# A state-space stage that scans four tokens per step instead of two, and moves its rows through a scratch in HBM

## The reference

```
def s5_mixer(h, a_re, a_im, log_dt, b_re, b_im, c_re, c_im, d_skip, w_glu):
    u = h.astype(jnp.float32).reshape(B, L, N_GROUPS_2, SSM_GROUP)
    dt = jnp.exp(log_dt.astype(jnp.float32))[:, None]
    decay = jnp.exp(a_re * dt)
    ab_re = decay * jnp.cos(a_im * dt)
    ab_im = decay * jnp.sin(a_im * dt)
    ...
    bb_re = coef_re * br - coef_im * bim
    bb_im = coef_re * bim + coef_im * br
    bu_re = jnp.einsum('blgc,gpc->blgp', u, bb_re)
    bu_im = jnp.einsum('blgc,gpc->blgp', u, bb_im)
    ...
    _, _, x_re, x_im = lax.associative_scan(_complex_scan_op, (ar, ai, bu_re, bu_im), axis=1)
    y = (jnp.einsum('blgp,gcp->blgc', x_re, c_re.astype(jnp.float32))
         - jnp.einsum('blgp,gcp->blgc', x_im, c_im.astype(jnp.float32)))
    y = y.reshape(B, L, D) + d_skip.astype(jnp.float32) * u.reshape(B, L, D)
    g = jax.nn.gelu(y).astype(h.dtype)
    ga, gb = jnp.split(g @ w_glu, 2, axis=-1)
    return ga * jax.nn.sigmoid(gb)
```

## Time and profile before

| | |
|---|---|
| median of 3 runs | 2961.07 us (2959.12 to 2964.72) |
| the profiled execution | 2959.73 us |
| its span in the trace | 2957.9 us |
| TensorE busy | 2792.2 us, 94% of the span |
| VectorE busy | 1404.8 us, 47% |
| GpSimd busy | 860.2 us, 29% |
| ScalarE busy | 539.1 us, 18% |

### The profile page before, as it was taken

One profiled execution on the slowest core, in us unless ns is written; L12 is line 12 of the kernel. 1 busy time (PEld: TensorE's weight loads), 2 busy tenths in 40 slices (PEclk: granted clock), 3 DMA queues, 4 the chain that ended last, 5 costly groups with the idle time before them and its releaser, 6 DMA issues.

```text
span 2957.9 us, 28891 instructions
## 1 busy us (share of the span) xinstructions
PE 2792.2 (94%) x11348; PEld 1991.8 (67%) x11348; DVE 1404.8 (47%) x2231; ACT 539.1 (18%) x1019; POOL 860.2 (29%) x688
## 2 busy tenths in 40 slices
PE   8999999999999999999999899999994469999999
PEld 7888884755448888875446547888442124688888
DVE  6454312166526544232496434555317991466521
ACT  2000000111101000011121522222015430222200
POOL 5444320000324444410000323442014650344432
PEclk9999999999999999997799999999996679999999
DMA  6555321211125454221011002224210002122222
GB/s 225 169 171 167 100 96 57 71 52 48 43 86 167 164 171 160 86 72 43 27 59 57 29 29 72 93 92 124 68 52 16 0 1 86 58 92 92 83 79 68
DMA packets 222626, 253.37 MB, mean 86 GB/s; under 512 B 16328, under 2 KB 209180, under 8 KB 222364
## 3 DMA queue, kind: packets, MB, share of 16 engines
q1 hardware_dynamic: 207996, 199.32, 20.9%
q10 hardware_dynamic: 14496, 52.21, 5.1%
HBM read 249.41 MB, written 2.10 MB: 85 GB/s over the span
## 4 chain that ended last, share of the span: by engine, by line
PE 83%; DVE 12%; ACT 2%; issue 1%; POOL 1%; SPq 0%; DMA 0%; DVEq 0%; POOLq 0%
PE ps L612 36%; PE ps L668 13%; PE ps L1134 9%; PE ps L498 5%; PE ps L1600 4%; PE ps L2271 4%; DVE phase L2429 2%; PE ps L1161 1%; PE ps L1641 1%; PE ps L1653 1%; DVE phase L2414 1%; PE ps L893 1%; PE ps L1269 1%; DVE rs L1850 1%; DVE act_t L2371 1%
## 5 line engine op out<-in xcount | busy, mean ns | idle before, releaser
L612 PE MATMUL ps<-hT,ring 128*128 128x256 f32 x2816 | 653.6, 380 | 3.8 <-ACT hT L1039 1.4
L612 PEld LDWEIGHTS ps<-hT,ring 128*128 128x128 f32 x2816 | 534.2, 190 | 80.9 <-issue 4.1
L612 PE MATMUL ps<-phase,ring 128*128 128x256 f32 x2112 | 498.5, 379 | 0.4 <-DVE phase L561 0.4
L540 POOL TENSOR_TENSOR ring<-ring 128x512 f32<-128x512 f32 (+1 forms) x124 | 161.1, 1299 | 1005.8 <-DMA ring<-in_ffn_w 515.2
L612 PEld LDWEIGHTS ps<-phase,ring 128*128 128x128 f32 x2112 | 400.4, 190 | 54.7 <-issue 0.8
L668 PE MATMUL ps<-phase,ring 128*128 128x256 f32 x1848 | 400.6, 379 | 1.0 <-issue 1.0
L668 PEld LDWEIGHTS ps<-phase,ring 128*128 128x128 f32 x1848 | 350.7, 190 | 48.8 <-issue 1.4
L1134 PE MATMUL ps<-hT,ring 128*128 128x512 f32 x512 | 227.9, 599 | 3.1 <-ACT phase L1326 2.5
L1600 PE MATMUL ps<-hT,ring 128*128 128x512 f32 x448 | 198.2, 599 | 0.9 <-ACT hT L1039 0.9
L543 POOL TENSOR_TENSOR ring<-ring 128x512 f32<-128x512 f32 (+1 forms) x124 | 191.1, 1541 | 0.0
L694 DVE TENSOR_TENSOR act_t<-u,ps 128x256 f32<-128x256 f32 x176 | 73.4, 421 | 235.6 <-PE ps L612 235.3
(11 more groups left out here) (333 smaller groups left out, 3141.2 us busy)
## 6 DMA issues: line engine op xcount, KB each, us to landing
ring<-in_ffn_w SPq DMA_DIRECT2D x60, 1024.0 KB, 5.2
ring<-in_ffn_w_up SPq DMA_DIRECT2D x44, 1024.0 KB, 5.1
phase<-in_ada_w ACTq DMA_DIRECT2D x64, 512.0 KB, 3.9
ring<-in_w_in SPq DMA_DIRECT2D x19, 1024.0 KB, 5.1
sq<-in_ada_w ACTq DMA_DIRECT2D x32, 512.0 KB, 4.1
ring<-in_attn_w_in SPq DMA_DIRECT2D x14, 1024.0 KB, 5.0
ring<-in_ffn_w_down SPq DMA_DIRECT2D x8, 1408.0 KB, 6.1
ring<-in_ssm_w_glu SPq DMA_DIRECT2D x8, 1024.0 KB, 5.5
```

The costliest lines, as they stand in the source:

```text
L540: pool.tensor_tensor(s1, a21, a22, ALU.add).then_inc(combined, 1)
L612: mm = pe.matmul(ps[:, 4 * w + bank_of[name], 0:HALF], left[:, c], right[name](c), start=(opens and c == 0), stop=(c == KC // 2 - 1), skip ...
```

## The change

One scan step covers four tokens: the stage has eight units of four pairs of groups, each 4 x 128 columns wide. What was the matrix `CB` becomes a direct matrix within a block of four tokens (`direct`, 64 by 64 per pair of groups), into which the skip term is folded. Its blocks are multiplied out by TensorE at hook (1,1), copied, and placed by 32 DMAs from SBUF to SBUF. The 64-row input of a unit is no longer stacked by ScalarE: SP stores each chunk of `hT` to a scratch in HBM and loads it back in eight pieces into `sq`; ScalarE stores the GELU of a unit to a second scratch, and SP loads it back in eight pieces into `hT`. Four chunks instead of six are multiplied early in the gated product. The small steps run on 64 partitions and there are 62 of them; B is loaded twice, in its second arrangement (`b_own`) into the unused tails of two ring slots, and C goes there too.

The diff, cut to its core:

```diff
-STEPS = np.broadcast_to(np.arange(2, T + 1, 2), (P, T // 2)).astype(np.float32)
+STRIDE = 4
+NK = T // STRIDE
+STEPS = np.broadcast_to(np.arange(STRIDE, T + 1, STRIDE), (P, NK)).astype(np.float32)
...
         def down_loads(sp, n, wd):
             for q in range(4):
+                if q == 2:
+                    ssm_c_loads(sp)
                 for s in range(2):
                     load_slot(sp, n + 2 * q + s,
...
-        NK = T // 2
-        SSM_UNITS = PAIRS // 2
+        GC = 16
+        SSM_UNITS = KC
...
+        def ssm_own_loads(sp):
+            sp.wait_ge(s_cz, 4)
             for n, name in enumerate(("ssm_b_re_2", "ssm_b_im_2")):
+                sp.dma_start(b_own[n], a[name][0].rearrange("(v j) s c -> (j s) v c", j=2)).then_inc(s_cin, 16)
+
+        def ssm_place_direct(sp):
+            sp.wait_ge(s_drow, 4)
+            sp.wait_ge(s_zero, 1)
...
+                            sp.dma_start(direct[to:to + GC, u:2 * KC:2, g, GC * l:],
+                                         direct_rows[src:src + GC, :, 0:GC * (STRIDE - l)]).then_inc(s_dir, 16)
...
+            if (q, half) == (0, 0):
+                pe.wait_ge(s_cz, 4)
+                for n in range(2):
+                    mm = turn(pe, cz_flat[n], 4 + 2 * n, KC)
+                mm.then_inc(s_par, 1)
...
+            if (q, half) == (1, 1):
+                pe.wait_ge(s_bz, BZ_STEPS)
+                pe.wait_ge(s_ca, CA_STEPS)
+                pe.wait_ge(s_cap, CA_STEPS)
+                for p in range(PAIRS):
+                    rows_of = slice(32 * (p % 4), 32 * (p % 4) + 32)
+                    for n in range(2):
+                        mm = pe.matmul(ps[rows_of, 6, (p // 4) * HD:(p // 4 + 1) * HD],
+                                       b_wide[n][:, p, :, :], CA[n][:, p, 0:4, :], start=(n == 0), stop=(n == 1))
+                mm.then_inc(s_par, 1)
...
         def ssm_matrices_dve(dve):
...
+            ssm_narrow(dve, 0, s_ca)
             n = 0
+            for i in range(STRIDE):
...
+            dve.wait_ge(s_bz, n)
+            dve.wait_ge(s_cin, 64)
             for k in range(2):
+                dve.memset(b_wide[k], 0.0).then_inc(s_bz, 1)
...
+                dve.tensor_tensor(bt[0], b_own[k], own_re, ALU.mult).then_inc(s_bz, 1)
+                dve.tensor_tensor(zt, b_own[1 - k], own_im, ALU.mult).then_inc(s_bz, 1)
...
+            ssm_ca(dve, 0, s_ca, s_cap)
...
         def ssm_glu_loads(sp):
             w = feat(a["ssm_w_glu_2"][0])
             for b in range(4):
+                if b == 2:
+                    ssm_moves(sp)
...
+            def store(c):
+                sp.wait_ge(h_ready, h_before(6) + c + 1)
+                sp.dma_start(u_dram[c], hT[:, c, :]).then_inc(s_urow[c % 2], 16)
+
+            def back(c):
+                sp.wait_ge(s_yrow[c % 2], 16 * (c // 2 + 1))
...
+            store(0)
+            store(1)
+            for c in range(KC):
+                sp.wait_ge(s_urow[c % 2], 16 * (c // 2 + 1))
+                if c >= 2:
+                    sp.wait_ge(s_bu, 2 * (c - 1))
...
+                if c + 2 < KC:
+                    store(c + 2)
+                if c >= 4:
+                    back(c - 4)
+            for c in range(KC - 4, KC):
+                back(c)
+
+        GLU_EARLY = 4
...
             if on(5):
+                ssm_own_loads(sp)
+                ssm_place_direct(sp)
                 ssm_glu_loads(sp)
```

More of the change, by code:

```diff
@@ L2180, in ssm_turned_act @@
+            if (q, half) in ((2, 0), (2, 1)):
+                n = half
+                pe.wait_ge(s_parc, 8 + 4 * n)
+                turn(pe, bz_flat[n], 4, 2 * KC).then_inc(s_par, 1)
+        PARC = 4 + 3 + 1 + 4 + 4
+        def ssm_turned_act(act, step):
+            act.wait_ge(s_par, step + 1)
+            if step == 0:
+                for n in range(2):
                     for b in range(2):
@@ new lines, in each @@
+            def each():
+                for t in range(4):
+                    for j in range(2):
+                        yield t, slice(64 * j, 64 * j + 64), slice(t * NK, (t + 1) * NK)
+            pe.wait_ge(s_zero, 3)
+            for c in range(SSM_UNITS + 2):
+                if c < SSM_UNITS:
+                    pe.wait_ge(s_stack[c % 2], 128 * (c // 2 + 1))
+                    if c >= 2:
+                        pe.wait_ge(s_pre, 4 * (c - 2) + 4)
+                    for n in range(2):
+                        for t, half, cols in each():
+                            pe.matmul(ps[half, 2 * (c % 2) + n, cols],
+                                      BT[n][half, 2 * c + t // 2, (t % 2) * HD:(t % 2 + 1) * HD],
+                                      stacked[half, c % 2, cols], start=True, stop=True)
+                    if c == 0:
+                        pe.wait_ge(s_dir, 16 * 32)
+                    if c == 2:
+                        pe.wait_ge(h_ready, h_before(6) + KC)
+                    if c >= 4:
+                        pe.wait_ge(s_g, c - 3)
+                    for t, half, cols in each():
+                        mm = pe.matmul(ps[half, 4 + (c + 2) % 4, cols], direct[half, 2 * c + t // 2, t % 2, :],
+                                       stacked[half, c % 2, cols], start=(t == 0), stop=False, skip_group_check=True)
+                        if t == 3:
+                            mm.then_inc(s_bu, 1)
+                if c >= 2:
+                    v = c - 2
```

480 lines of the change are left out of this document (249 added, 231 removed).

## The result

The changed kernel takes **2910.5 us** (median of 4 runs, 2909.6 to 2911.8) against 2960.1 us for the kernel before in the same session: ratio 0.983, 95% interval 0.9813 to 0.9847. The forecast was 2921 us in a range of 2900 to 2948. Direction and range held; the gain is 49.6 us where 39 were forecast. The profiled execution took 2910.84 us around a span of 2909.0.

The account below looks back on a forecast made before the run. VectorE was taken to bound the scan loop and TensorE everything else. The terms -90.6 + 5.2 + 8.0 + 4.1 + 34.3 sum to -39.0 us, giving 2921 us, range 2900 to 2948, chance 0.80.

Parts of the forecast that it names:

- Term 1: Scan loop, first rotation to end of last back rotation: eight units instead of sixteen, 101.2 us against 191.8, -90.6 us.
- Term 2: Start of the scan stage: chunk through HBM in eight pieces, then small products, before the first rotation; +5.2 us.
- Term 3: End, last back rotation to gated product: GpSimd's last operation, matmuls, GELU, store and eight loads, 12.7 us against 4.7; +8.0 us.
- Term 4: Gated product: four more records behind the wait (1.7 us) and a resume at low clock after idling (2.4); +4.1 us.
- Term 5: Preparation under the down projection: TensorE waits 29.1 us at hook (1,1) for late `b_own` and VectorE's steps; +34.3 us in all.
- Tiles run in pairs: First rival denied this: 64 by 64 tiles don't overlap, TensorE needs 17.1 us per unit and bounds the loop; 2955 us, chance 0.08.
- The moves did not bound: Second rival claimed they do: SP's 17 DMAs per unit bound the loop; gain gone over 1.07 us each, 3127 at 2.30; chance 0.06.
- The rule that the prediction set against the change: Skill's 2.0 us fixed per DMA; the unit's 17 paid one after another: 35 us per chunk, kernel about 3097 us.
- The preparation was not hidden by itself: Third rival claimed it stays hidden: `b_own` comes early enough, no wait at the hook, 31.5 us less; 2889 us, chance 0.06.

## Why the prediction held, and where it was off

**The sum.** The five terms were too high by 15.3 us together (8.6, 0.4, 1.8, 0.3 and 4.2 in their order), and 5.4 us that no term had, ahead of the down projection and behind the gated product, went the other way. That the sum was off by 9.9 us only is in part luck.

**Bounds.** VectorE bounds the loop and TensorE the preparation, as forecast: 89.6 of 90 us, and a wait of 27.2 us at hook (1,1), which two edits to queues took away.

**Term 1, 8.6 us too small a gain.** First iteration 4.5 us (forecast 5.1), five of 12.04 (13.3), two of 10.1 (10.7), last 7.7 (8.2). Two terms were mis-sized. Eight scans take 3.69 us, not 4.1: a step of the argument had failed, "rotations and scans keep their pace beside GpSimd". Rotations do. Scans do not. Alone, a scan of 128 columns starts 0.315 us behind the one before it, and 1.0 us of the eight is a wait for GpSimd's second addition. Before it was the same. Two neighbouring scans of the kernel before, timeline:

```profile
2286.36 1.69 DVE L2429 TENSOR_TENSOR_SCAN phase<-phase 128x256 f32<-128x256 f32 x1
2287.97 0.66 DVE L2429 TENSOR_TENSOR_SCAN phase<-phase 128x256 f32<-128x256 f32 x1
```

Free scans of 256 columns start 0.58 us apart, and one in four waits 1.0 us, so the 0.87 that I split into a fixed and a per-column part was a mean over three free scans and one held up. The fixed part is 0.05 (0.315 for 128, 0.58 for 256), not 0.13. Second, fractions and back rotation take 5.95 us, not 6.7. The prediction had one VectorE operation slip in at each of GpSimd's; that holds, but all three that slip in are now fractions of 0.3 us, where before one fraction and two back rotation operations did, and the back rotation comes when GpSimd is done.

What rows show of the rule is this: a VectorE operation with two inputs in SBUF that is issued while GpSimd computes on inputs in SBUF ends only when GpSimd's operation has; rotations, with one input in PSUM, run on. So do operations beside a GpSimd clear, which reads nothing. In the preparation of the changed kernel, timeline:

```profile
2113.30 0.68 DVE L2301 TENSOR_TENSOR act_t<-phase 128x512 f32<-128x512 f32 x1
2116.13 1.54 DVE L2301 TENSOR_TENSOR act_t<-phase 128x512 f32<-128x512 f32 x1
...
2112.83 1.81 POOL L2598 MEMSET phase<- 128x2048 f32 x1 [0.94 <-DVE phase L2209]
2115.61 1.50 POOL L2221 TENSOR_TENSOR act_t<-phase 128x512 f32<-128x512 f32 x1
```

The Trainium skill (SBUF — State Buffer, SBUF: two separate sides) says just that: the two share a pair of ports as an exclusive lock for the whole instruction, which a VectorE operation with two SBUF inputs needs against a GpSimd operation that reads SBUF. The trace agrees in every case above, scans (1.42 against 0.39), fractions (1.34 against 0.32) and products (1.75 against 0.68) on the one side, rotations (0.68 in both) and the operation beside the clear (0.68) on the other.

**Term 2, right in the sum by luck.** From the ready chunk to the first rotation it is 11.5 us, not 13.2. Store and eight pieces take 7.2 us from chunk to first product (forecast 8.1): landings are 2.1 and 1.8 us, not 2.4. The products take 4.3, not 5.1, at a granted clock of 0.67; in two variants with the same code, where it was 0.55 and 0.50 over them, they took 5.2 and 5.5, so 5.1 was a fair price for the low level. Against this gain of 1.7 us stand 1.3 that no term had, ahead of the ready chunk: 0.4 for the norm's slower first step and 0.9 before it, where TensorE's small products for the norm ran at a granted clock of 0.69 instead of 1.00. (ScalarE's short copies were eight per chunk, not 16; no term used the number.)

**Term 3.** GpSimd's last operation 1.0 and handoffs, 32 records 1.97 (2.5), then store to flow 7.1 (8.1): all small, all the same way.

**Term 4.** As forecast within 0.3; the gated product waited on the last chunk alone. TensorE had idled 4.7 us, not 8, and the granted clock was 0.50 all the same in the 4 us behind it.

**Term 5.** The landing took 10.6 + 0.3 us (2148.07 to 2159.01), not 13.4; VectorE 15.8 us as forecast (15.7); matmuls 3.66 (3.5). The resume cost 0.2 instead of 2.4: the granted clock is 0.50 in the first 4 us and 0.95 in the next, but the small matmuls fill those 4 us, and 44 records of the down projection then take 19.08 us where 18.9 is the pace. A resume was charged twice, in the low-clock price of the matmuls and again.

**Rivals.** Tiles run in pairs. The moves did not bound: an issue is 0.45 us beside everything else, never near the 1.07 from which they would decide, and SP's 17 issues of a unit overlap with the landings. The rule that the prediction set against the change, some 2 us fixed per DMA, comes near what each landing shows (1.8 us for 32 KB, 2.1 for 256 KB), but it is latency, paid twice at the start and twice at the end (store and load), not per piece. The preparation was not hidden by itself; hiding it was priced at 31.5 us and gave 29.0.

## What to carry to other kernels

Where VectorE bounds, a second engine's help has to be priced at what it locks: here GpSimd took three operations of 0.61 us off VectorE and cost it 3.0 us in an iteration, so giving them back took 6.6 us off the loop (8.7 by the medians), and moving one GpSimd operation under VectorE's reads of PSUM took off another 6.0 (7.0). When a mean duration is to be split into parts, look at the single instructions first; a stall in one of four looks like a price of all. And a load's place in a queue can cost more than the work it feeds: 29 of the 30 us that the preparation grew by were two positions.

## What the runs showed that was not expected

- Where both read SBUF, VectorE (two inputs there) and GpSimd hold each other up one whole operation at a time, in both directions, scans too (1.42 us against 0.39). Rotations with one input in PSUM (0.68) and operations beside GpSimd's clear (0.68) are exempt.
- A scan alone starts every 0.315 us at 128 columns and every 0.58 at 256: halving the width and doubling the number costs 9%.
- SP's issue of a DMA has no fixed price: 0.45 us for 32 KB pieces and 0.42 for the 256 KB store between them in one kernel, 0.34 for both 16 KB pieces and the same store in another.
- The norm's step of 512 columns takes 1.03 us instead of 0.67 where it reads every fourth float32 of both inputs, the residual chunk in SBUF and the norm's factor in PSUM; which of the two costs it was not tried.
- The same start took 13.4 to 14.6 us in ten kernels. Its first products took 4.3 us at a granted clock of 0.67, and in two other kernels 5.2 at 0.55 and 5.5 at 0.50.
- 64 by 64 tiles at opposite corners overlap even where the instructions of one corner come in a row: 256 records in 31.6 us against 25.4 alternated.
